# Normalising the next chunk's tokens ahead of the conv products, from more buffers, in the first stage of a hybrid attention and conv layer

## What is computed

```
hn   = x * rsqrt(mean(x*x) + 1e-6) * norm_g
proj = hn @ w_in                                   # 1024 -> 9216
q, k, v, z_a, hc, gb, gc, z_b, g = split(proj)
attn = 3 head groups, dilation 1, 4 and 16; keys at 0, +-d .. +-64 d; ALiBi; mixed by log-sum-exp
a    = (silu(z_a) * attn) @ w_attn_out
u    = gc * hc
conv = w0 * u[t-1] + w1 * u[t] + w2 * u[t+1]
c    = (silu(z_b) * (gb * conv)) @ w_conv_out
out  = x + (sigmoid(g_a) * a + sigmoid(g_c) * c) @ w_o      # then a final RMSNorm
```

## Time and profile before

| | us |
|---|---|
| median of the runs (3 runs, lowest 1525.01) | 1525.6 |
| the profiled execution, its own time | 1522.79 |
| its span, slowest core (core 1) | 1521.2 |
| spans of the eight cores | 1511.1 to 1521.2 |
| PE (TensorE) busy, core 1 | 1471.3 (97%) |
| DVE / ACT / POOL busy, core 1 | 848.5 / 686.3 / 192.1 |

### The profile page before, as it was taken

One profiled execution on the slowest core, in us unless ns is written; L12 is line 12 of the kernel. 1 busy time (PEld: TensorE's weight loads), 2 busy tenths in 40 slices (PEclk: granted clock), 3 DMA queues, 4 the chain that ended last, 5 costly groups with the idle time before them and its releaser, 6 DMA issues.

```text
span 1521.2 us, 30871 instructions; the slowest of 8 cores (1511.1 to 1521.2 us)
## 1 busy us (share of the span) xinstructions
PE 1471.3 (97%) x13381; PEld 858.1 (56%) x13381; DVE 848.5 (56%) x1089; ACT 686.3 (45%) x1034; POOL 192.1 (13%) x364
## 2 busy tenths in 40 slices
PE   6889999999999999999989999999999999999996
PEld 5645675565665544444444877768676544444443
DVE  4556256346365588544466446557384696533455
ACT  4665455555565323433342456566574321222222
POOL 3332000000000011211122100000000101000011
PEclk9989999999999999999999999999999999999998
DMA  8585223224144154433397443333333322222157
GB/s 201 140 172 110 57 53 69 39 67 68 26 93 60 36 87 102 97 63 64 65 251 241 109 85 64 63 77 53 69 61 50 50 49 54 39 34 42 21 204 238
DMA packets 92648, 133.97 MB, mean 88 GB/s; under 512 B 52065, under 2 KB 52193, under 8 KB 92514
## 3 DMA queue, kind: packets, MB, share of 16 engines
q1 hardware_dynamic: 67170, 85.86, 20.9%
q0 software_dynamic: 25344, 46.15, 20.4%
HBM read 145.97 MB, written 23.66 MB: 112 GB/s over the span
## 4 chain that ended last, share of the span: by engine, by line
PE 89%; DMA 7%; DVE 2%; ACT 1%; issue 1%; POOL 0%; SPq 0%; POOLq 0%; ACTq 0%; DVEq 0%
PE ps L442 81%; PE ps L454 8%; DMA Y<-xw 4%; DMA wbf<-wblk 1%; DVE Y L406 1%; PE ps L469 1%; DMA y<-Y 1%; ACT hnT L429 0%; DVE hnT L430 0%; ACT Y L393 0%; POOL wbf L473 0%; ACT Y L429 0%; DVE Y L430 0%; POOL stat L416 0%; POOL stat L593 0%
## 5 line engine op out<-in xcount | busy, mean ns | idle before, releaser
L442 PE MATMUL ps<-hnT,wbf 128*128 128x512 bf16 (+5 forms) x5776 | 1033.6, 336 | 13.4 <-DMA wbf<-wblk 4.3
L442 PEld LDWEIGHTS ps<-hnT,wbf 128*128 128x128 bf16 x5776 | 528.7, 98 | 456.3 <-issue 10.1
L393 ACT ACTIVATE Y<-ps 128x1024 bf16<-128x1024 f32 (+2 forms) x296 | 242.5, 863 | 194.1 <-PE ps L442 131.8
L429 ACT ACTIVATE Y<-ps 128x512 bf16<-128x512 f32 (+2 forms) x342 | 202.5, 595 | 261.7 <-PE ps L442 245.2
L397 DVE TENSOR_TENSOR Y<-ps,Y 128x512 f32<-128x512 f32 (+1 forms) x200 | 126.2, 663 | 293.4 <-PE ps L454 253.3
L406 DVE SCALAR_TENSOR_TENSOR Y<-Y,ps 128x512 f32<-128x512 f32 x192 | 131.3, 685 | 212.3 <-PE ps L442 160.8
L473 POOL DMA_DIRECT2D wbf<-wblk x160 | 90.3, 567 | 915.9 <-PE ps L442 887.3
L393 ACT ACTIVATE Y<-ps,cf 128x512 f32<-128x512 f32 x128 | 87.4, 686 | 194.6 <-PE ps L442 188.2
L393 ACT ACTIVATE Y<-Y 128x1024 bf16<-128x1024 f32 x80 | 84.5, 1056 | 143.5 <-DVE Y L406 86.5
L397 DVE TENSOR_TENSOR Y<-Y,et 128x1024 bf16<-128x1024 bf16 x192 | 130.4, 684 | 10.1 <-ACT Y L393 5.6
L454 PEld LDWEIGHTS ps<-Y 64*128 64x128 bf16 x4640 | 114.4, 94 | 33.9 <-issue 27.8
(11 more groups left out here) (25 smaller groups left out, 421.5 us busy)
## 6 DMA issues: line engine op xcount, KB each, us to landing
wbf<-wblk POOLq DMA_DIRECT2D x160, 256.0 KB, 4.8
Y<-xw SPq DMA_DIRECT2D x56, 512.0 KB, 5.9
y<-Y SPq DMA_DIRECT2D x32, 512.0 KB, 5.0
Y<-xw SPq DMA_DIRECT2D x48, 256.0 KB, 4.3
Y<-wblk POOLq DMA_DIRECT2D x16, 256.0 KB, 5.3
et<-etab SPq DMA_DIRECT2D x8, 384.0 KB, 6.0
cv<-Y SPq DMA_DIRECT2D x4, 768.0 KB, 5.8
Y<-cv SPq DMA_DIRECT2D x4, 768.0 KB, 5.8
```

The lines of the kernel that those rows point to most:

```text
L393: R.add("act", [lambda e: e.activation(out=out.a, in_=in_.a, func=func, scale=scale, **kw)], c_act(in_.n) + (0.2 if accum is not None else ...
L429: return e.activation(out=out.a, in_=in_.a, func=AF.Copy)
L442: fns = [(lambda e, m=m: e.matmul(m[0].a, lhsT=m[1].a, rhs=m[2].a, start=m[3], stop=m[4])) for m in mms]
```

## The change

In the first stage the own tiles of chunk c + 1 (for the last chunk: the four span tiles) come in program order after `chunks[c]` and ahead of `conv_chunk(c)`. The own tiles have seven x buffers (three more at 84, 88 and 92 KB of the work area, where two small start-up tiles lay that move to 96 and 100 KB) and the least recently used one is taken; there are three bf16 buffers for all tiles of the stage. The halo tiles come after steps 1 and 3 of unit 0 and steps 0 and 1 of unit 1. The planner's cost of a DVE instruction becomes 0.16 + 0.00107 n us (it was 0.15 + 0.00105 n), and two copies lose their special lower cost: that to `hnT` (0.69 us) and that of the first unit's transposed values. No instruction of the engines is added or taken out.

```
+        xt0e = xt0 + [yb(k, 4096, F32) for k in (84, 88, 92)]
-        xn0 = [yb(24 + 2 * i, 2048, BF16) for i in range(2)]
+        xn0 = [yb(24 + 2 * i, 2048, BF16) for i in (0, 1, 3)]
...
         def c_dve(n):
-            return 0.15 + n * 0.00105
+            return 0.16 + n * 0.00107
...
-        lnc = {"i": 0}
+        lnc = {}
+
+        def oldest(bufs):
+            b = min(bufs, key=lambda b: lnc.get(b, 0))
+            lnc[b] = 1 + max(lnc.values(), default=0)
+            return b
...
-            i = lnc["i"]
-            lnc["i"] += 1
-            xt, xn = xts[i % len(xts)], xns[i % len(xns)]
+            xt, xn = oldest(xts), oldest(xns)
...
-                copy(hnT.ap(hcol, [[WIN, 8]] + hd), pb.ap(pcol, [[128, 8]] + pd), dcost=0.69 / len(dsts))
+                copy(hnT.ap(hcol, [[WIN, 8]] + hd), pb.ap(pcol, [[128, 8]] + pd))
...
-                    xt0, xn0, gb0, jk0, bank)
+                    xt0e, xn0, gb0, jk0, bank)
...
-                         pb.ap(0, [[128, n], [64, 2], [1, 64]]), dcost=0.15 + 0.00053 * 128 * n)
+                         pb.ap(0, [[128, n], [64, 2], [1, 64]]))
...
-                    if u == 0 and more:
-                        more[c]()
+                    if (u, c) in more:
+                        more[u, c]()
...
-        grow, one = yb(80, 4096, F32), yb(84, 512, F32)
+        grow, one = yb(96, 4096, F32), yb(100, 512, F32)
...
-            for p in range(4 * c, 4 * c + 4):
-                if c:
-                    ln_own(p, ln_bank())
             for f in chunks[c]:
                 f()
+
+            for j in range(4):
+                if c < 3:
+                    ln_own(4 * c + 4 + j, ln_bank())
+                else:
+                    ln_span(j, (48, 192), 16, ln_bank())
             conv_chunk(0, 0, c, conv_buf[1], c < 2)
         R.tag = "start4"
-        for c in range(4):
-            ln_span(c, (48, 192), 16, ln_bank())
...
-            attention(h, [halo(c) for c in range(4)] if h == 0 else ())
+            attention(h, {uc: halo(c) for c, uc in enumerate(((0, 1), (0, 3), (1, 0), (1, 1)))} if h == 0 else ())
```

## The result

The changed kernel takes 1514.87 us (median of 4 runs, 1513.59 to 1516.99) beside 1525.3 us of the kernel before (lowest 1522.97): 10.4 us less, ratio 0.9938 with a 95% interval of 0.9919 to 0.9958. The forecast was 17.8 us less, 1508 us, with 1500 to 1514 us as its likeliest range: the measured time lies 0.9 us above that and inside the wider 1497 to 1523 us.

What follows compares the result with a forecast made beforehand. PE bounds the kernel; only 27.4 us of waiting and low clock between 26.3 and 145.5 us could go. Terms 10.3 + 7.8 - 0.3 = 17.8 us gave 1508 us, likeliest 1500 to 1514, wider 1497 to 1523.

Steps and rivals of the forecast that it cites:

- the first term: New order and buffers, 26.3 to 102.2 us: 10.3 us won out of 17.9 us of waiting and low clock.
- The losses kept there: Up to 102.2 us, 7.6 us stay: 1.2 early, 1.8 in `start4`, 3.1 for span pairs, 1.5 low clock.
- the signs listed as right: Earlier chunks 2 and 3, first scores near 92 us, PEclk 1.00, transpose wait under 4 us, PE 100% after unit 0.
- the first sign listed as wrong: New waits of the transposes inside chunk 3's conv products or in units 0 and 1, behind ACT waiting for x.
- the halo term: Halo tiles spread over units 0 and 1: 7.8 us won of unit 0's 9.5 us of waiting and low clock.
- covered: The six halo tiles moved to unit 1 hide beside PE, busy 39.9 of 39.9 us; DVE 10.2, ACT 19.8.
- the price of lost cover: If a halo tile came late for unit 2's first products: a paired wait of 3.1 to 6.3 us.
- The weights: x loads pulled forward meet the first weight loads: 0.3 us lost, bounds 0 and 2.2 us.
- The planner's costs: New choice of ACT or DVE for copies, whole program: nothing, bounds plus and minus 3 us.
- Transposes that wait in front of products: Rival: products stand behind late transposes of eight paired tiles; up to 1549 us, chance of slower 0.05.
- The clock does not come back: Rival: mean clock stays at 0.89, only waiting is won, 1516 us; chance 0.18 shared with half the gain.
- Half the gain: Rival: order moves waiting, gaps stay in each stretch, 1512 or 1520 us; chance 0.18 shared with no clock.

Runs made afterwards that it cites:

- e8: The kernel before with the new program order alone (old buffers, old costs, halo tiles in unit 0): 1516.1 us.
- e11: The kernel before with seven x and three bf16 buffers, least recently used first, and nothing else: ratio 0.9996 to the kernel before.
- e1: The changed kernel with all twelve halo tiles back in unit 0: 1513.96 us.
- e2: The kernel before with nothing but the halo tiles spread over units 0 and 1: 1528.56 us.
- e6: The changed kernel with two more x buffers for the halo tiles of chunks 2 and 3: 1510.78 us.
- e3: The changed kernel with the planner's DVE costs of before, including the two special copy costs: 1513.79 us.
- e4: The changed kernel with the second load of every paired tile no longer waiting for the first to land: 1506.24 us.
- e9: The changed kernel with all second loads freed and two more x buffers for the late halo tiles: ratio 0.9808 to the kernel before.
- e10: The changed kernel with second loads freed, two more x buffers and the planner's x loads landing after 6 us: ratio 0.9835 to the kernel before.
- e7: The changed kernel with the planner told that x loads land 6 us after their transfer instead of 2 us: 1509.92 us.
- e5: The changed kernel with second loads freed only for the 16 tiles of half 1: 1509.32 us.

## Why the prediction was right, and where it was off

**The direction and the mechanism of the first term hold.** PE waited at the chunk borders because the transposes stood behind the products. e8 shows that the order alone removes most of it, e11 that the buffers alone remove nothing; together they win 13.3 us up to the first scores (median of the cores), where the term was 10.3 us. The losses kept there were too large on core 1: the paired span loads, put at 3.1 us, cost at most the 1.9 us that PE waits in that stretch, and the low clock went altogether. Of the signs listed as right all came on that core but one: the stretch after unit 0 no longer has PE at 100% (26.86 of 31.32 us). And the first sign listed as wrong came as well, new waits of the transposes in units 0 and 1 behind ACT waiting for x.

**That the time stayed inside the wider range is partly luck.** The first term was 3.0 us too small, which made up for a part of the halo term, below, 7.8 us too large. From the first scores to u2.0 the changed kernel loses 1.3 of its 13.3 us and after that 1.6 us more, which leaves the 10.4 us measured, 58% of the 17.8 us forecast.

**The halo term failed: forecast 7.8 us won, measured nothing** (e1 beside the changed kernel: 0.9 us the other way; e2: no gain in the time and 5.2 us lost by u2.0). The step that failed is "covered". It weighed busy shares of DVE and ACT, and these do have room in unit 1: DVE 14.75 and ACT 15.16 of 31.32 us. What ran out is x buffers. The halo tiles have four; each comes free only after a normalisation, which needs a bf16 buffer, which needs the transposes of the halo tiles before; spread out, these transposes come late, and the last loads with them. The prediction named the price of lost cover, 3.1 to 6.3 us; it was 4.5 us of waits and 3.0 us of low clock behind them. e6 shows the cause: with two more x buffers and nothing else PE has no gap in unit 1. (Whether more bf16 buffers would have done the same was not tried.)

**The weights** came 0.7 us later on core 1, where 0.3 was taken and 0 to 2.2 were the bounds. Over the cores there is no delay: on the seven of each profile where the chain of waits shows it, the last of the first weights lands at 26.3 to 27.4 us before and 26.3 to 27.3 after, median 26.9 both times. By the rule of the Trainium skill ("DMA: Bandwidth & Descriptors", "Issuing engines are not separate DMA queues") the term would have been the upper bound, 2.2 us; the traces do not show that.

**The planner's costs** at nothing: e3 confirms it (1.1 us between the medians, inside the spread of either). Waits in the output stage, 6.5 us where 4.8 were, took back about 1.6 us of the 12.0 us that u2.0 had won; they lie inside the 3 us allowed for the later stages.

**The rivals.** "Transposes that wait in front of products" happened for the last halo tiles in unit 1, not for all eight tiles counted, and by late buffers more than by paired loads: freeing the pairs moves u2.0 by 1.5 us (e4). "The clock does not come back" is refuted: from 26.98 to 86.14 us PE is busy 93 to 98% on the eight cores and the mean PEclk is 1.00 on four of them and 0.94 to 0.97 on the others, where the kernel before had 0.88 to 0.96 at 84 to 90% (26.3 to 102.2 us). The Trainium skill's limit of 13/16 for dense matmuls on three or more cores of a die ("TensorE: Matmul & The Clock Gate", Part 1, "Seeing it yourself") does not show there. "Half the gain" gave 1512 to 1520 us, and 1514.9 us lies there. Its mechanism holds in part: the order did move waiting, but not so that gaps stay in each stretch; nearly all of it went up to the first scores and new waiting arose in units 0 and 1.

**One reading of the rows was off.** In the earlier trace rows PE falls under 9 in the first three slices, once in the middle and in the last, not in four and two; nothing in the sum rests on it.

**Open.** What the wait for ACT near the first scores (4.6 us in the changed kernel) costs in the end. That squares waiting for x stood ahead of ready evacuations is shown by e9 and e10, which differ by one number of the planner: with it the wait goes. But other waits came in its place, in e10 for a weight block and in e7 for normalised tiles, and no run is faster by its absence.

## What to carry to other kernels

Count buffers and the chain that frees them, not only busy shares, before calling moved work covered: an engine with half its time free still waits if the load behind it cannot be issued. In a list that is fixed in advance, an instruction that waits for a transfer should not stand ahead of the evacuations that the bottleneck needs; but taking such a wait away wins time only if the next one is not right behind it (e10). And look at what a dependency tracker cannot see: two loads into different partitions of one buffer were serialised here, and undoing that (e4) brought 8.6 us, nearly as much as the change itself, 5.5 of them far from the place of the change (e5).

## What the runs showed that was not expected

A 512 KB load of x has a median of 5.9 us from issue to landing over the whole span of the kernel before; in unit 1, beside a store of K, half of such a load took 8.34 us in the changed kernel (the chain of waits above). The planner counts 2.85 us for that half (0.85 us of transfer and 2 us to land), so it was over 5 us late. And a wait of 4.5 us on PE is followed by 3 us of work lost to the lower clock: the price of these gaps was about one and two thirds of what the waits alone say.
